# A sliding-window attention mixer that packs two key blocks into one probability tile

## The reference, cut to what matters

```python
# each 128-query block reads its own and the previous 128-key block
rel = QBLK + a_idx - j_idx                       # a: query 0..127, j: key 0..255
valid = (rel >= 0) & (rel < C_WINDOW) & (key_pos >= 0)      # C_WINDOW = 128
bias = jnp.where(valid, alibi, MASK_VALUE)
s = einsum('bqhgd,bkhd->bhgqk', qi, kb) * scale + bias
m = maximum(max(s, axis=-1), sink)
p = exp(s - m)
denom = sum(p, axis=-1) + exp(sink - m)
return einsum('bhgqk,bkhd->bqhgd', p / denom, vb)
```

## Time and profile before

| | us |
|---|---|
| median of 3 runs | 1869.99 |
| the profiled execution, its own time | 1870.26 |
| its span in the profile | 1868.5 |
| TensorE busy in the span | 1858.9 (99%) |
| second mixer, round 0 to the last `values` | 572.2 to 672.4 |

### The profile page before, as it was taken

The page is one execution under the profiler, slowest core; times in us unless marked ns, Lnnn a source line. Parts: engine busy times, 40 slices in busy tenths (PEclk is TensorE's granted clock), DMA queues, the critical chain, the costliest instruction groups (busy, mean ns, idle before and its releaser), DMA issues.

```text
span 1868.5 us, 24518 instructions
## 1 busy us (share of the span) xinstructions
PE 1858.9 (99%) x9034; PEld 1499.5 (80%) x9034; DVE 1186.3 (63%) x1828; ACT 803.2 (43%) x1215; POOL 152.2 (8%) x111
## 2 busy tenths in 40 slices
PE   9999999999999999999999999999999999999999
PEld 7777888888887788888888887888777788888887
DVE  5686676356647866763576498675666667644762
ACT  5475443233436754332344343422577554322341
POOL 1132000000021020000000101121210010000000
PEclk9999999999999999999999999999999999999999
DMA  6211222322231122323322322445333222223223
GB/s 220 85 52 68 90 97 83 112 91 104 77 109 49 69 69 93 110 68 113 106 89 85 115 90 93 147 137 186 126 127 113 69 90 90 86 94 113 90 79 101
DMA packets 39521, 185.99 MB, mean 100 GB/s; under 512 B 4448, under 2 KB 5856, under 8 KB 24848
## 3 DMA queue, kind: packets, MB, share of 16 engines
q1 hardware_dynamic: 39152, 184.77, 29.0%
q10 hardware_dynamic: 288, 0.16, 0.0%
HBM read 176.42 MB, written 8.49 MB: 99 GB/s over the span
## 4 chain that ended last, share of the span: by engine, by line
PE 93%; DVE 4%; ACT 2%; issue 1%; DMA 1%; POOL 0%; SPq 0%; DVEq 0%; ACTq 0%; POOLq 0%
PE banks L771 55%; PE banks L1320 22%; PE banks L818 5%; PE banks L1234 1%; PE banks L1259 1%; PE banks L1245 1%; PE banks L1368 1%; DVE w_lo L2056 1%; PE banks L1397 1%; DVE tmp L2436 1%; ACT w_hi L1474 1%; PE banks L1380 1%; PE banks L1333 1%; PE banks L991 1%; PE banks L1130 0%
## 5 line engine op out<-in xcount | busy, mean ns | idle before, releaser
L771 PE MATMUL banks<-xn_hi,w_hi 128*128 128x512 f32 x1208 | 467.2, 390 | 0.5 <-DVE big L2154 0.5
L771 PE MATMUL banks<-xn_hi,w_lo 128*128 128x512 f32 x1208 | 466.1, 389 | 0.0
L771 PE MATMUL banks<-xn_lo,w_hi 128*128 128x512 f32 x1208 | 466.0, 389 | 0.0
L1474 ACT ACTIVATE w_hi<-raw 128x2048 fp32r<-128x2048 f32 (+2 forms) x134 | 228.3, 1704 | 226.8 <-PE banks L771 188.9
L2056 DVE TENSOR_TENSOR w_lo<-raw,w_hi 128x2048 fp32r<-128x2048 f32 (+2 forms) x134 | 273.5, 2041 | 48.5 <-ACT w_hi L1474 48.0
L771 PEld LDWEIGHTS banks<-xn_hi,w_hi 128*128 128x128 f32 x1208 | 226.8, 188 | 49.0 <-issue 1.4
L771 PEld LDWEIGHTS banks<-xn_lo,w_hi 128*128 128x128 f32 x1208 | 226.8, 188 | 47.4 <-issue 0.5
L771 PEld LDWEIGHTS banks<-xn_hi,w_lo 128*128 128x128 f32 x1208 | 226.8, 188 | 47.1
L1540 ACT ACTIVATE tmp<-scaled_h,par 128x512 f32<-128x512 f32 x132 | 100.5, 809 | 349.8 <-DVE scaled_h L2112 349.8
L2112 DVE TENSOR_TENSOR scaled_h<-banks,token_rs 128x512 f32<-128x512 f32 x132 | 85.0, 686 | 183.3 <-PE banks L771 166.0
L1320 PE MATMUL banks<-xn_hi,w_hi 128*128 128x512 f32 x400 | 161.2, 403 | 0.6 <-DVE big L2162 0.6
(11 more groups left out here) (302 smaller groups left out, 2646.3 us busy)
## 6 DMA issues: line engine op xcount, KB each, us to landing
raw<-weights SPq DMA_DIRECT2D x114, 1024.0 KB, 4.9
raw<-weights SPq DMA_DIRECT2D x24, 768.0 KB, 4.3
raw<-weights SPq DMA_DIRECT2D x24, 640.0 KB, 3.9
big<-scratch SPq DMA_DIRECT2D x40, 256.0 KB, 4.5
att<-scratch SPq DMA_DIRECT2D x16, 256.0 KB, 3.9
scratch<-stage SPq DMA_DIRECT2D x12, 256.0 KB, 4.6
scratch<-con SPq DMA_DIRECT2D x12, 256.0 KB, 2.2
raw<-weights SPq DMA_DIRECT2D x4, 512.0 KB, 3.7
```

Of the source, the lines that this page charges most:

```text
L771: return pe.matmul(psum[:, 2 * p + m, :], w[:, at_:at_ + P], x_part(k), start=start, stop=stop)
L1474: act.activation(w_hi[:, sl], raw[:, sl], ACT.Identity).then_inc(hi_done, 1)
```

## The change

The row buffer of a tile still takes 256 negated scores. A new VectorE operation takes the elementwise minimum of its two 128-wide halves, which leaves the one valid key of each pair j, j + 128 (a "packed" tile). From there on all is 128 wide: the exponential, the scaling, the transpose (one per query block and head, two per `turn` half), and the copy. The value product then uses p·v(previous block) over the whole packed tile plus (masked p)·(v(current) − v(previous)): the triangular mask keeps the entries that belong to the current block. So `v_diff` is formed once, and a masked copy of each transposed tile is made by VectorE in `masked(r-2)`, which stands in round r behind `maxima(r)`; `values(r-2)` waits for it. The ALiBi bias is made by ScalarE behind `copy`, no longer by VectorE. `exps` wait for the packed tile.

```diff
                 def turn(r):
                     for m in range(2):
                         pe.wait_ge(c_fin, 2 * r + m + 1)
...
-                        for b, i, w in c_blocks(r):
-                            for j in range(256 - w, 256, P):
-                                last = pe.transpose(psum[:, 6 + m, 256 * b + j:256 * b + j + P], c_prob(m, r, b)[:, j:j + P], ident)
+                        for b in range(2):
+                            last = pe.transpose(psum[:, 6 + m, b * P:(b + 1) * P], c_prob(m, r, b)[:, P:2 * P], ident)
...
                     pe.wait_ge(c_copied, 2 * r + 2)
+                    pe.wait_ge(c_masked, 2 * r + 2)
                     for b, i, w in c_blocks(r):
-                        first = max(i - 1, 0)
-                        for j in range(first, i + 1):
+                        parts = [(vtok[0], max(i - 1, 0), b * P)] + ([(v_diff, i - 1, (2 + b) * P)] if i else [])
+                        for n, (v, j, from_) in enumerate(parts):
...
                 def exps(r):
...
-                            act.wait_ge(c_max, n)
-                            pr = c_prob(m, r, b)[:, 256 - w:257]
+                            if i:
+                                act.wait_ge(c_pack, c_packs(r, m, b))
+                            else:
+                                act.wait_ge(c_max, 4 * r + 2 * m + 1)
+                            pr = c_prob(m, r, b)[:, P:2 * P + 1]
...
                 def copy(r):
-                        act.activation(c_slot(m, r)[:, c0:T], psum[:, 6 + m, c0:T], ACT.Identity).then_inc(c_copied, 1)
+                        act.activation(c_slot(m, r)[:, 0:2 * P], psum[:, 6 + m, 0:2 * P], ACT.Identity).then_inc(c_copied, 1)
+                def alibi(it, m):
+                    if it >= 2:
+                        act.wait_ge(c_max, 8 * (it - 1))
+                    act.activation(c_bias[it % 2][:, 256 * m:256 * m + 256], ccol("window", 0, 256), ACT.Identity,
+                                   scale=ccol("c_slope", 2 * it + m)).then_inc(c_biased, 1)
...
                         copy(r - 1)
+                    if r // 2 + 1 < C_PAIRS:
+                        alibi(r // 2 + 1, r % 2)
...
                 def maxima(r):
                         me.wait()
+                        dve.wait_ge(c_biased, 2 * it + 2)
...
+                    for m in range(2):
+                        dve.wait_ge(c_max, 4 * r + 2 * m + 2)
+                        for b, i, w in c_blocks(r):
+                            if i:
+                                pr = c_prob(m, r, b)
+                                dve.tensor_tensor(pr[:, P:2 * P], pr[:, 0:P], pr[:, P:2 * P], ALU.min).then_inc(c_pack, 1)
...
-                            pr = c_prob(m, r, b)[:, 256 - w:256]
+                            pr = c_prob(m, r, b)[:, P:2 * P]
...
+                def masked(r):
+                    b0 = 1 - r % 2
+                    for m in range(2):
+                        dve.wait_ge(c_copied, 2 * r + m + 1)
+                        dve.tensor_tensor(c_slot(m, r)[:, (2 + b0) * P:T] ..., c_slot(m, r)[:, b0 * P:2 * P] ...,
+                                          ccol("tri", 0, P) ..., ALU.mult).then_inc(c_masked, 1)
...
+                dve.tensor_tensor(v_diff[:, 0:3 * P], vtok[0][:, P:T], vtok[0][:, 0:3 * P], ALU.subtract).then_inc(c_v, 1)
...
                     if r < C_ROUNDS:
                         maxima(r)
+                    if r >= 2:
+                        masked(r - 2)
                     if r % 2 == 1 and r // 2 + 1 < C_PAIRS:
                         scaled(1 + r // 2 + 1)
...
-                    if r // 2 + 1 < C_PAIRS:
-                        alibi(r // 2 + 1, r % 2)
```

More of the change, by code:

```diff
@@ L302, in blocks_program @@
         c_turned_v, c_v = sem("c_turned_v"), sem("c_v")
+        c_pack, c_masked, c_biased = sem("c_pack"), sem("c_masked"), sem("c_biased")
         c_scored, c_max, c_exp, c_fin = sem("c_scored"), sem("c_max"), sem("c_exp"), sem("c_fin")
@@ L465, in c_prob, with c_packs @@
             return att[:, bass.ds(7 * T + 320 * (4 * (r % 2) + 2 * b + m), 320)]
+        v_diff = chunk(att, 3)
+        def c_packs(r, m, b):
+            return 6 * (r // 2) + (m + 1 if r % 2 == 0 else 2 + 2 * m + b + 1)
         def c_lo_chunk(it):
@@ L1386, in values @@
                         if it == 0:
-                            pe.wait_ge(c_v, 1)
+                            pe.wait_ge(c_v, 2)
                         else:
@@ L1390, in values @@
                     pe.wait_ge(c_copied, 2 * r + 2)
+                    pe.wait_ge(c_masked, 2 * r + 2)
                     for b, i, w in c_blocks(r):
-                        first = max(i - 1, 0)
-                        for j in range(first, i + 1):
+                        parts = [(vtok[0], max(i - 1, 0), b * P)] + ([(v_diff, i - 1, (2 + b) * P)] if i else [])
+                        for n, (v, j, from_) in enumerate(parts):
                             for m in range(2):
                                 at_ = j * P + 64 * m
-                                from_ = 256 * b + 256 - w + (j - first) * P
-                                last = pe.matmul(psum[64 * m:64 * m + 64, 2, i * P:(i + 1) * P], vtok[0][:, at_:at_ + 64],
+                                last = pe.matmul(psum[64 * m:64 * m + 64, 2, i * P:(i + 1) * P], v[:, at_:at_ + 64],
                                                  c_slot(m, r)[:, from_:from_ + P],
-                                                 start=(i == 0), stop=(i == 3 and j == 3), skip_group_check=True)
+                                                 start=(i == 0), stop=(i == 3 and n == 1), skip_group_check=True)
                     last.then_inc(c_pv, 1)
@@ L1754, in copy @@
                 def copy(r):
-                    c0 = P if r % 2 == 0 else 0
                     for m in range(2):
@@ L1773, in c_stage @@
                 act.activation(vtok[0], psum[:, 2, :], ACT.Identity).then_inc(c_v, 1)
+                alibi(0, 0)
+                alibi(0, 1)
                 norm_job(1)
@@ L2352, in finish @@
                         for b, i, w in c_blocks(r):
-                            pr = c_prob(m, r, b)[:, 256 - w:256]
+                            pr = c_prob(m, r, b)[:, P:2 * P]
                             last = dve.tensor_scalar(pr, pr, row_inv[:, 2 * i + m:2 * i + m + 1], None, ALU.mult)
                         last.then_inc(c_fin, 1)
+                def masked(r):
+                    b0 = 1 - r % 2
+                    for m in range(2):
+                        dve.wait_ge(c_copied, 2 * r + m + 1)
+                        dve.tensor_tensor(c_slot(m, r)[:, (2 + b0) * P:T].rearrange("p (j l) -> p j l", j=2 - b0),
+                                          c_slot(m, r)[:, b0 * P:2 * P].rearrange("p (j l) -> p j l", j=2 - b0),
+                                          ccol("tri", 0, P).rearrange("p (o l) -> p o l", o=1).to_broadcast([P, 2 - b0, P]), ALU.mult).then_inc(c_masked, 1)
                 def square_rest(n):
@@ L2377, in c_stage @@
                 scaled(1)
-                alibi(0, 0)
-                alibi(0, 1)
                 evacuate(q, 0)
@@ L2382, in c_stage @@
                 evacuate(q, 1)
+                dve.wait_ge(c_v, 1)
+                dve.tensor_tensor(v_diff[:, 0:3 * P], vtok[0][:, P:T], vtok[0][:, 0:3 * P], ALU.subtract).then_inc(c_v, 1)
                 for r in range(C_ROUNDS + 2):
```

5 lines of the change are left out of this document (removed).

## The result

The changed kernel took 1876.92 us in the median of 6 runs (1876.24 to 1878.11), the kernel before 1870.1 on the same chip (1869.86 to 1870.62): a ratio of 1.0035 with a 95% interval of [1.0025, 1.0046], slower by 6.8 us. The forecast was 1875.0 and slower, with a range of 1873.7 to 1877; the median lies 0.08 us under the upper end of it, and three of the six runs above that end. The profiled execution took 1876.24 us for a span of 1874.4, which is 5.98 more than the one before.

The account below looks back on a forecast made before the run. TensorE, busy 99% of the span, was taken as the bound, with VectorE having no slack in the mixer. Waits of 10.4 us, less 0.2 there before and 5.2 saved, gave +5.0: 1875.0 us, range 1873.7 to 1877.

Parts of the forecast that it names:

- The saving on TensorE: In the second mixer's turns, 64 transposes instead of 112, at 0.109 us each, save 5.2 us.
- VectorE's load: In the mixer, packs at 0.20 us and wide masks at 0.33 raise VectorE's busy time from 82 us to 93.
- Nothing overlaps: Rival: VectorE's small operations cost their full length, 0.28 and 0.42 us; +9.0 us, 1879.0; chance 0.06.
- at the same 0.30: ScalarE in the mixer: the bias moved there has a spacing of 0.30 us, as a 256-wide copy.
- The waits: TensorE stands for masks, output halves, scaled queries, finish and a weight split in the mixer: 10.4 us, 0.2 there before.
- scaling gets narrower, 0.20 each: VectorE in the mixer: scalings become 128 wide with a spacing of 0.20 us instead of 0.265 at 256.
- Cover holds: Rival: VectorE's packs and masks cost only the low end in the mixer; 1870.4 to 1872.4 us; chance 0.38.
- TensorE's saving decides: Rival: in the mixer only TensorE's 5.2 us saving shows, 1864.8; -1.7 us with packs and masks at zero cost; chance 0.04.
- What would show it: Signs in the new profile: 64 transposes, about 7 us of weight-load waits at values, VectorE busy about 93 us, mixer some 105.

Follow-up runs that it names:

- e1: The changed kernel without packs and masked copies, exponentials as wide and early as before (does not compute the mixer): 4.6 us faster than the kernel before.
- e8: The kernel before with only its bias moved to ScalarE: +0.77 us in the mixer, about 1 us by the medians, interval including no change.
- e10: The changed kernel with GpSimd's square of chunk 4 held until finish of round 3 has ended: scalings 0.88 us instead of 1.45, but the time did not fall.
- e9: The changed kernel with its packs moved behind the exponentials, which are early and wide again: median +5.8 us against the kernel before, +4.42 in the mixer.
- e5: The kernel before plus VectorE's time for the packs, as instructions behind the maxima for which nobody waits: +1.9 us.
- e11: The changed kernel with the masked copies formed by GpSimd instead of VectorE: +7.16 us against the kernel before.

## Why the prediction was right, step by step

**The number.** The mechanism and the places held. That the median fell into the range was partly luck: it lies 1.9 above the 1875.0, 0.08 inside the end, and the misses in size nearly all went the same way, towards too little waiting.

**The saving on TensorE.** 5.2 us forecast. e1 shows 4.6, with 0.55 of waiting in it at the output half. Right.

**VectorE's load.** Spacings of 0.20 and 0.33 forecast, 0.203 and 0.335 measured; 93 us busy, 93.00 measured. The full length (286 and 418 ns), by which *Nothing overlaps* was reckoned, is what each lasts, not what it costs the engine.

**ScalarE.** The bias "at the same 0.30" was wrong: it lasts 500 ns and has a spacing of 0.40 (589.61 to 590.01 on ScalarE's timeline). The row that I took it from (382 ns) reads a bank of PSUM and has no scale operand; this one reads SBUF and a scale for each partition. Rows of the changed kernel, all the same function on 128x512, tell the two apart:

```profile
L1485 ACT ACTIVATE xn_hi<-x,par 128x512 fp32r<-128x512 f32 x40 | 28.7, 717 | 39.5 <-DVE x L2183 10.0 <-DVE x L2326 9.9 <-DVE x L2734 9.9
...
L1882 ACT ACTIVATE mix_hi<-big 128x512 fp32r<-128x512 f32 x8 | 4.8, 624 | 1.3 <-DVE big L2614 1.2
...
L1777 ACT ACTIVATE big_r<-banks 128x512 fp32r<-128x512 f32 x8 | 4.7, 592 | 5.0 <-PE banks L1403 5.0
...
L1615 ACT ACTIVATE big_r<-banks,par 128x512 fp32r<-128x512 f32 x4 | 2.7, 676 | 0.0
```

The scale costs 93 ns from SBUF (717 against 624) and 84 from PSUM (676 against 592), the source in SBUF 32 to 41, so most of the difference is the scale operand. e8 puts the whole move at +0.8 to +1.1.

**The waits.** Compared by the distance between the starts of stages, as they were walked, less the undisturbed distance. (The idle time in brackets is shorter by 0.06 or more, since the instruction ahead is counted to its end.) In round 7, for example, 617.77 to 619.60 less 0.54 is 1.29.

```
round               2     3     5, 9   6     7     10    11    12    13
walked             2.84  0.52  0.10   0.69  0.79  0.90  1.36  1.66  0.61
measured           3.11  1.12  0.16   0.70  1.29  0.90  1.39  1.69  0.66
```

Every place is right, and so are nearly all sizes. Two are off, rounds 3 and 7, by 0.60 and 0.50. This is the term that was mis-sized: "scaling gets narrower, 0.20 each". In these rounds four scalings take 1.45 us and not 0.88, as GpSimd's square runs beside them (589.16 to 591.11, and 613.67 to 615.09). e10 took the square away in round 3, and the stretch went; the wait went too, about half of it by the estimate at e10 and the rest by TensorE's slow clock. The row was there to be read before: VectorE's timeline of the kernel before has

```profile
589.31 1.58 DVE L2354 TENSOR_SCALAR att<-att,small 128x128 f32<-128x128 f32 x4
```

where the earlier trace rows has the same four at 1.01, and its GpSimd

```profile
588.14 1.95 POOL L706 TENSOR_TENSOR tn<-big 128x512 f32<-128x512 f32 x1 [14.05 <-DVE big L2305]
```

I had taken the spacing from a round in which nothing disturbed it. Rounds 5, 9 and 11 are stretched too (1.67 us at 600.72 and at 625.29, 1.45 at 638.25), and there something else comes last. The two rounds make 1.1 of the 1.46 us between the walked 5.0 and the mixer's +6.46; round 2, 0.27 longer than walked over its three waits, is most of what is left.

The Trainium skill (SBUF — State Buffer, section "Who interferes with whom") says that VectorE and GpSimd share one pair of ports under an exclusive lock, and that a VectorE instruction with two inputs in SBUF contends with a GpSimd one that reads SBUF. It names tensor_scalar among the operations that can take the pair, in their two-port modes. The traces agree for tensor_tensor (0.49 to 1.33 us in e9) and for the scalings (0.88 to 1.45), and the square itself lasts 1.04 alone and 1.95 where the weight split of 1.22 us runs when it starts.

**The rest.** About 0.8 us lies between +5.98 in the profile and +6.8 in the medians. The profile was the quickest of the six runs. The one run whose mean clock shows a fall took 1877.05, and the two slowest, 1877.68 and 1878.11, read 1.000, so such a fall does not account for them. What does stays open.

**The rivals.** *Cover holds* is out: e5 shows how it could have looked (+1.9 for the packs' load) had nothing waited for the packs. *TensorE's saving decides* needs packs and masks away, and then it is indeed -4.6 (e1); it was put at -1.7 with only their cost at zero and the exponentials late. *Nothing overlaps* came nearest of the rivals in time, 1879.0, 2.1 above the measured median where the forecast is 1.9 below it; the time alone hardly tells them apart, and the spacings of 0.203 and 0.335 refute its mechanism.

**What would show it.** The forecast looked for the waits in the weight-load queue. They are there for the output halves (4.1 us at L1403), but those for the masked copies stand in the matmuls' own group, 5.8 us, since the masked copy is the moving operand of these products and not the weight.

## What to carry to other kernels

An engine with 18% idle time can absorb most of the work that nobody waits for, and can't absorb a wait: the same packs cost 1.9 us as load and 7.7 when the next engine waited for them. Before moving an instruction between engines, look at what stands behind it in the queue that receives it, not at the busy shares. Take each spacing from the round in which it will count, and look on GpSimd's timeline for what runs beside it. Where a saving needs help from a nearly full engine, take it only in the places where that engine has time: seven chosen rounds of 16, with packs, bias and one square placed better, gave -2.0 us, where all 16 gave +6.8 as first placed and +5.8 with the packs placed better (e9).

## What the runs showed of the hardware

- GpSimd's square (128x512 tensor_tensor) and VectorE's scalings or two-input tensor_tensor hold one another up until about when the first is done: four scalings went from 0.88 to 1.45 us (gone again in e10, where the square was moved), two packs from 0.49 to 1.33 us (e9), and 32 masks on GpSimd raised the mean scaling from 333 to 453 ns (e11).
- A wait of 1.56 us of TensorE was followed in e10 by some 3 us at a granted clock of 0.50, at a price of 1.55 us, and one of 1.67 us in e11 by one of 1.59; waits of 1.55 and 1.62 us at the same places of the changed kernel's profile were not.
- An activation of 128x512 lasts 624 ns from SBUF and 592 from PSUM, and 717 and 676 ns with a scale read for each partition. The 128x256 bias has both, 500 ns, where the copy from PSUM has neither, 366.
- VectorE's small operations in a row start closer together than they last: 0.203 us for 286 ns (128 wide), 0.335 for 418 (256 wide).
